# Decay rows of a Mamba-2 mixer copied to all partitions by bf16 products, with its convolutions first, and one bank read early in the mixer before it

## What is computed

```python
proj = h @ w_in                         # (1024, 7432)
ya = swa_sink_attention(...)            # A: sliding window attention
yb = hgrn2_mixer(...)                   # B: gated linear recurrence
yc = mamba2_mixer(...)                  # C: state space model
yd = forgetting_attention(...)          # D
g = jax.nn.sigmoid(gate).reshape(bsz, seq, N_BRANCH, D_MODEL)
merged = g[:, :, 0] * (ya @ w_br_a) + g[:, :, 1] * (yb @ w_br_b) + g[:, :, 2] * (yc @ w_br_c) + g[:, :, 3] * (yd @ w_br_d)
return merged @ w_out
```

```python
conv = causal_conv(xbc, conv_w, width 4, per channel) + conv_b
xbc = jax.nn.silu(conv)                 # 512 channels: xs, bs, cs
a_cum = jnp.cumsum(a * dt, within a chunk)
lmat = jnp.exp(a_cum[l] - a_cum[s])     # for s <= l
y_diag = jnp.einsum('bclhn,bcshn,bhcls,bcshp->bclhp', cc, bc, lmat, xc)
```

## Time and profile before

| | us |
|---|---|
| median of three runs | 2283.86 |
| lowest and highest | 2280.04 and 2293.8 |
| the profiled execution, its own time | 2281.75 |
| its span, first to last instruction | 2280.0 |
| TensorE busy | 2161.1 (95% of the span) |
| VectorE busy | 869.4 (38%) |
| ScalarE busy | 413.2 (18%) |
| GpSimd busy | 590.3 (26%) |
| TensorE's granted clock, mean | 0.979 |

### The profile page before, as it was taken

The page is one execution under the profiler, slowest core; times in us unless marked ns, Lnnn a source line. Parts: engine busy times, 40 slices in busy tenths (PEclk is TensorE's granted clock), DMA queues, the critical chain, the costliest instruction groups (busy, mean ns, idle before and its releaser), DMA issues. The chain is left out here.

```text
span 2280.0 us, 22500 instructions
## 1 busy us (share of the span) xinstructions
PE 2161.1 (95%) x7446; PEld 1146.1 (50%) x7447; DVE 869.4 (38%) x1964; ACT 413.2 (18%) x895; POOL 590.3 (26%) x520
## 2 busy tenths in 40 slices
PE   7999999999989999999999999999999999999990
PEld 4548466557446456544444555444444444444440
DVE  4000024555452323311112666464444444444425
ACT  2100023433422212111111122011111111111112
POOL 0700000122000100012223000355544444454524
PEclk9999999999989999999999999999999999999995
DMA  5411101010211111152213302689999999999953
GB/s 136 138 42 49 40 28 38 28 38 28 66 47 42 65 47 61 32 186 68 70 46 117 124 37 89 263 311 347 343 349 350 352 352 347 342 344 352 335 154 148
DMA packets 126441, 361.93 MB, mean 159 GB/s; under 512 B 33948, under 2 KB 65808, under 8 KB 100896
## 3 DMA queue, kind: packets, MB, share of 16 engines
q1 hardware_dynamic: 100768, 306.35, 36.4%
q0 software_dynamic: 23520, 54.61, 9.5%
q10 hardware_dynamic: 2080, 0.01, 0.1%
HBM read 315.22 MB, written 65.01 MB: 167 GB/s over the span
## 5 line engine op out<-in xcount | busy, mean ns | idle before, releaser
L285 PE MATMUL banks<-arena 128*128 128x512 f32 x1568 | 724.2, 601 | 16.7 <-ACT arena L329 10.5
L2651 PE MATMUL banks<-arena 128*128 128x512 f32 x1056 | 472.2, 600 | 5.7 <-DVE arena L2644 2.8
L285 PEld LDWEIGHTS banks<-arena 128*128 128x128 f32 x1568 | 287.7, 193 | 311.6 <-issue 289.4
L2630 POOL DMA_INDIRECT arena<-h_rows,index x268 | 278.0, 1037 | 340.2 <-DVE index L2616 278.5
L2651 PEld LDWEIGHTS banks<-arena 128*128 128x128 f32 x1056 | 196.4, 191 | 231.6 <-issue 229.8
L2667 PE MATMUL banks<-arena 128*128 128x512 f32 x528 | 242.7, 602 | 1.3 <-ACT arena L2469 0.8
L2667 PEld LDWEIGHTS banks<-arena 128*128 128x128 f32 x528 | 95.4, 190 | 97.3 <-issue 95.6
L1622 PE MATMUL banks<-arena 128*128 128x512 f32 x320 | 141.7, 597 | 2.7 <-DVE arena L1651 2.7
L2638 POOL DMA_INDIRECT sums<-arena,row_to x66 | 109.4, 1657 | 104.1 <-DMA sums<-arena,row_to 54.3
L2644 DVE STREAM_TRANSPOSE arena<-arena 128x1024 f32<-128x1024 f32 x66 | 133.5, 2023 | 6.3 <-PE banks L2651 6.3
L291 PE MATMUL banks<-arena 128*128 128x256 f32 (+1 forms) x640 | 128.0, 359 | 0.0
(11 more groups left out here) (358 smaller groups left out, 2132.4 us busy)
## 6 DMA issues: line engine op xcount, KB each, us to landing
arena<-in_w_exp_gate_dram SPq DMA_DIRECT2D x66, 1024.0 KB, 7.0
arena<-in_w_exp_up_dram SPq DMA_DIRECT2D x66, 1024.0 KB, 10.1
arena<-in_w_exp_down_dram SPq DMA_DIRECT2D x66, 1024.0 KB, 14.0
arena<-in_w_in_dram SPq DMA_DIRECT2D x26, 1024.0 KB, 5.3
gates<-arena SPq DMA_DIRECT2D x48, 256.0 KB, 2.0
arena<-gates SPq DMA_DIRECT2D x48, 256.0 KB, 2.6
arena<-h_rows,index POOLq DMA_INDIRECT x268
arena<-in_x_dram SPq DMA_DIRECT2D x8, 512.0 KB, 5.8
```

The costliest lines, as they stand in the source:

```text
L285: mm = pe.matmul(bank[0:width], w[:, q, col:col + width], g.hT[:, q, at * HALF:(at + 1) * HALF], start=(q == 0), stop=(q == KT - 1))
L2630: return pool.indirect_dma_start(w.x[k][:, 256 * q:256 * (q + 1)], None, rows, bass.IndirectOffsetOnAxis(ap=g.index[:, k, q:q + 1], axis=0 ...
L2651: mm = pe.matmul(g.bank[:, 2, :].rearrange("p (a f) -> p a f", a=2), xT[:, k, :], wgu[:, :, k, :], start=(k == 0), stop=(k == KT - 1))
```

## The change

Four things, all inside `mixers`:

1. In B, `read_beside()` stands ahead of ScalarE's wait for the scans instead of behind it.
2. In C, VectorE makes three of the four convolutions ahead of the decay rows, the fourth behind the selectors. ScalarE reads the first unit before the first tanh, and the second after the third tanh.
3. The decay rows are split by GpSimd into three bf16 pieces whose sum is exact; they lie on partitions 0 to 7, 32 to 39 and 64 to 71 of `pieces`, with zeros between. The selectors are bf16 too, and three times as many.
4. The products at lines 1337 and 1343 become bf16 products over 96 partitions.

```diff
@@ mix_b, scalar
+        read_beside()
         act.wait_ge(scanned, 2)
-        read_beside()
         exps(0)
@@ mix_c
-    sel, sel2 = g.region(at + 4096, 4, P)[0:8], g.region(at + 4608, 2, P)[0:8]
+    sel = g.region(at + 4096, 256).bitcast(BF16).rearrange("p (h n) -> p h n", h=4)
+    sel2 = g.region(at + 4352, P).bitcast(BF16).rearrange("p (h n) -> p h n", h=2)
+    third = (slice(0, 8), slice(32, 40), slice(64, 72))
+    pieces = g.region(R3, HALF).bitcast(BF16)
+    middle, left = g.region(R3 + HALF, HALF).bitcast(BF16)[0:8], g.region(R3 + 1027, T)[0:8]
@@ gpsimd
+        pool.memset(sel[0:96], 0.0).then_inc(s["split"], 1)
+        pool.memset(sel2[0:96], 0.0).then_inc(s["split"], 1)
+        pool.wait_ge(s["conv"], 8)
+        pool.memset(pieces[0:96], 0.0).then_inc(s["split"], 1)
+        pool.wait_ge(s["summed"], 1)
+        pool.wait_ge(s["split"], 3)
+        pool.tensor_copy(pieces[third[0]], dec_rows).then_inc(s["split"], 1)
+        pool.wait_ge(s["split"], 4)
+        pool.tensor_tensor(left, dec_rows, pieces[third[0]], ALU.subtract).then_inc(s["split"], 1)
+        pool.wait_ge(s["split"], 5)
+        pool.tensor_copy(middle, left).then_inc(s["split"], 1)
+        pool.wait_ge(s["split"], 6)
+        pool.tensor_copy(pieces[third[1]], middle).then_inc(s["split"], 1)
+        pool.wait_ge(s["split"], 7)
+        pool.tensor_tensor(pieces[third[2]], left, middle, ALU.subtract).then_inc(s["split"], 1)
+        pool.wait_ge(s["split"], 8)
         pool.wait_ge(s["silu"], 3)
@@ scalar
-        for i in range(4):
+        def tanh(i):
             act.wait_ge(s["conv"], 4 * (i + 1))
             act.activation(th[:, i, :], xc[:, i, :], ACT.Tanh).then_inc(s["tanh"], 1)
-            stage((i + 1) // 2)
+        stage(1)
+        for i in range(3):
+            tanh(i)
+        stage(2)
+        tanh(3)
@@ vector (convolve(i) is the body of the old loop over i)
+        for i in range(3):
+            convolve(i)
         dve.wait_ge(s["z1"], 1)
@@
+        dve.wait_ge(s["split"], 2)
+        for r in third:
+            dve.tensor_copy(sel[r], bcast(g.ident[0:8, 0:4].unsqueeze(2), [8, 4, P])).then_inc(s["sel"], 1)
+            dve.tensor_copy(sel2[r, :, 0:HD], bcast(g.ident[0:8, 0:2].unsqueeze(2), [8, 2, HD])).then_inc(s["sel"], 1)
+            dve.tensor_copy(sel2[r, :, HD:P], bcast(g.ident[0:8, 2:4].unsqueeze(2), [8, 2, HD])).then_inc(s["sel"], 1)
+        convolve(3)
@@ tensor
-        pe.wait_ge(s["sel"], 3)
+        pe.wait_ge(s["sel"], 9)
+        pe.wait_ge(s["split"], 8)
@@
-                mm = pe.matmul(bank[:, 1, h * P:(h + 1) * P], sel[:, h, :], tile(dec_rows, m),
+                mm = pe.matmul(bank[:, 1, h * P:(h + 1) * P], sel[0:96, h, :], tile(pieces, m)[0:96],
@@
-                mm = pe.matmul(bank[:, 2, r * P:(r + 1) * P], sel2[:, r, :], tile(dec_rows, m),
+                mm = pe.matmul(bank[:, 2, r * P:(r + 1) * P], sel2[0:96, r, :], tile(pieces, m)[0:96],
```

More of the change, by code:

```diff
@@ L1125, in mix_c @@
     ss = g.sb("ssC", [P, NT, 2])
-    g.sel_rows = sel
-    names = ("halved z0 z1 z2 z3 z4 nl rowsd keepd summed sel colsT colsr conv tanh silu cpad clear tmT tmr xdt "
+    names = ("z0 z1 z2 z3 z4 nl rowsd keepd summed split sel colsT colsr conv tanh silu cpad clear tmT tmr xdt "
              "rowsb eb0 CB E eb att cdec xdec y u st skip yr gt s1 s2 sq ss sse ssq ssr n1 yT yTr").split()
@@ L1220, in vector, with convolve @@
         dve.tensor_scalar(g.rows[:], g.rows[:], g.rowbias[:], neg_row, ALU.add, ALU.mult).then_inc(s["z1"], 1)
+        dve.tensor_scalar(g.convw[:], g.convw[:], 0.5, None, ALU.mult).then_inc(s["z0"], 1)
+        dve.tensor_scalar(g.convb[:], g.convb[:], 0.5, None, ALU.mult).then_inc(s["z0"], 1)
+        dve.wait_ge(s["z0"], 4)
+        def convolve(i):
+            dve.tensor_scalar(xc[:, i, :], g.cX[:, i, 0:T], g.convw[:, i, 0:1], g.convb[:, i:i + 1],
+                              ALU.mult, ALU.add).then_inc(s["conv"], 1)
+            for t in range(1, 4):
+                dve.wait_ge(s["conv"], 4 * i + t)
+                dve.scalar_tensor_tensor(out=xc[:, i, :], in0=g.cX[:, i, t:t + T], scalar=g.convw[:, i, t:t + 1],
+                                         in1=xc[:, i, :], op0=ALU.mult, op1=ALU.add).then_inc(s["conv"], 1)
+        for i in range(3):
+            convolve(i)
         dve.wait_ge(s["z1"], 1)
@@ L1233, in vector @@
         dve.tensor_tensor_scan(dec_rows, keep, dec_rows, 0.0, ALU.mult, ALU.add).then_inc(s["summed"], 1)
-        dve.tensor_copy(sel, bcast(g.ident[0:8, 0:4].unsqueeze(2), [8, 4, P])).then_inc(s["sel"], 1)
-        dve.tensor_copy(sel2[:, :, 0:HD], bcast(g.ident[0:8, 0:2].unsqueeze(2), [8, 2, HD])).then_inc(s["sel"], 1)
-        dve.tensor_copy(sel2[:, :, HD:P], bcast(g.ident[0:8, 2:4].unsqueeze(2), [8, 2, HD])).then_inc(s["sel"], 1)
-        dve.tensor_scalar(g.convw[:], g.convw[:], 0.5, None, ALU.mult).then_inc(s["halved"], 1)
-        dve.tensor_scalar(g.convb[:], g.convb[:], 0.5, None, ALU.mult).then_inc(s["halved"], 1)
-        dve.wait_ge(s["halved"], 2)
-        for i in range(4):
-            dve.tensor_scalar(xc[:, i, :], g.cX[:, i, 0:T], g.convw[:, i, 0:1], g.convb[:, i:i + 1],
-                              ALU.mult, ALU.add).then_inc(s["conv"], 1)
-            for t in range(1, 4):
-                dve.wait_ge(s["conv"], 4 * i + t)
-                dve.scalar_tensor_tensor(out=xc[:, i, :], in0=g.cX[:, i, t:t + T], scalar=g.convw[:, i, t:t + 1],
-                                         in1=xc[:, i, :], op0=ALU.mult, op1=ALU.add).then_inc(s["conv"], 1)
+        dve.wait_ge(s["split"], 2)
[4 more added lines that the diff above has]
+        convolve(3)
         for i in range(4):
```

## The result

The changed kernel takes 2263.91 us (median of 4 runs, 2263.72 to 2266.67), the kernel before beside it 2285.45 (median of 4, 2280.04 to 2293.8): a ratio of 0.9895, with a 95% interval of 0.9872 to 0.9918. It is 1.05% faster by that ratio; the interval, 0.82 to 1.28%, holds 1% inside it. The two medians are 21.5 us apart, 0.94%.

What follows compares the result with a forecast made beforehand. TensorE, busy for 95% of the span, was taken to bound the kernel. C's head 9.3 plus C's loop 8.7 minus B's 4.1 gave 13.9 us less: 2267.9 profiled, 2270.0 as median, range 2261 to 2277.

Steps and rivals of the forecast that it cites:

- faster by over 1%: Whole kernel: a gain of about 22.8 us, distinguishable from no change; chance 0.04, against 0.93 same and 0.03 slower.
- B, the table load: Mixer B: the exponential's table load falls behind the wait for `gap_min`, so `scores(0)` comes 1.3 us later.
- B, the clock: Mixer B: TensorE idles 446.0 to 454.4, its clock is low when `scores(0)` starts, 2.8 us lost in the open.
- C's head: Mixer C before its loop: 9.3 us gained, 13.0 without GpSimd's split blocking VectorE by 6.5 to 8.3 us.
- Rival 1: No exclusion between GpSimd and VectorE: the split hides, C's head gains 13.0, about 2265 us; chance 0.22.
- The third unit, a wait of 1.8 to 3.6 us near 645: C's head: TensorE's `fill(14)` waits for `stage(4)` to read the third unit, held up by the fourth convolution.
- The second rival: Exclusion, and the clock falls in C: head gains 4.7 to 6.5 us, about 2274 us; chance 0.2.
- The fourth rival: GpSimd slow in bf16: the split takes 25 us, C's head loses 7 to 9, 2287 to 2291 us; chance 0.04.
- Short waits are free: TensorE's waits like the 2.2 us one cost no low clock; so none counted in C's head, 2.8 us if wrong.
- Behind C I count no change: After mixer C: everything hangs on C's end in the same way, so 0 us difference.
- The loop: C's loop: six float32 products per tile become bf16, saving 1.03 to 1.13 us a tile, 8.7 us taken.
- The third rival: C's loop: small bf16 products bound by weight loads, loop saves 0 to 3 us, about 2277 us; chance 0.04.

Runs made afterwards that it cites:

- table free: Changed kernel, early read kept, without the wait for the second scan ahead of B's exponential: 2265.49 us, ratio 0.9911 to the kernel before.
- bf16 only: Changed kernel with C's old order of convolutions and B's read late again; bf16 products and GpSimd split kept: 2283.76 us, ratio 0.9993 to the kernel before.
- filled kernel: Changed kernel with B's filling work redistributed, two units read early, no wait for the second scan: 2250.1 us, ratio 0.9821 to the kernel before.
- Late read: Changed kernel with B's read put back behind the wait for the scans, C's edits kept: 2261.83 us, ratio 0.9905 to the kernel before.
- before again: The kernel before, word for word, profiled a second time: 2287.35 us, ratio 0.9998.
- split on VectorE: Changed kernel with B's read late and the split's five instructions moved from GpSimd to VectorE: 2262.46 us, ratio 0.9881 to the kernel before.
- changed again: The changed kernel, word for word, run once more: 2265.73 us, ratio 0.9900 to the kernel before.
- order only: Changed kernel with float32 decay-row copies, no split, and B's read late; C's new order kept: 2274.87 us, ratio 0.9950 to the kernel before.
- selectors first: Changed kernel with B's read late and the nine selector copies ahead of the decay rows' scan: 2266.83 us beside 2289.56 for the kernel before.
- filled with the split on VectorE: The filled kernel with the split's five instructions moved from GpSimd to VectorE: 2251.57 us, ratio 0.9832 to the kernel before.
- one piece: Changed kernel with B's read late and the split cut to its first instruction, losing precision: 2255.54 us beside 2289.56 for the kernel before.

## Why the prediction was right, and where it was not

The changed kernel took 2263.91 us where I gave 2270.0 and a range of 2261 to 2277. The sign of each of the three terms was right; the sum fell 1.2 us short in the profile, and "faster by over 1%", to which I gave 0.04, can't be told from "the same" (0.82 to 1.28%). That the profile's sum came so close is partly luck: the loop gained 1.8 us more than its term, and D's end lost 1.65 for which I had no term.

**B, the table load: right.** It starts at 449.36 behind line 972, and `scores(0)` comes 1.33 us later; table free takes it back.

**B, the clock: right in size** (3.00 and 3.34 in two profiles, 2.72 in the kernel before with the early read; I had 2.8). The idle time of 8.4 us was 8.53. The row behind it is the earlier trace rows, and the reading that slow entries once covered by a wait would come into the open held.

**C's head: right in size (9.97 against 9.3), wrong in place.** I let VectorE's end move by the split, 6.5 to 8.3 us; it moved by 6.0 (8.2 us for nine copies that take 2.1 alone). But I said that the fourth convolution would grow by some 5 us, and it kept its 3.93: the split was over when it came, because the nine copies, which I had costed at 1.8 us, took all of the blocking. The Trainium skill, "SBUF — State Buffer", "Who interferes with whom", says of copies and casts that they too can take the shared pair, in a mode that uses two ports, and the one that comes second is blocked wholly. I had thought there of instructions with two inputs alone; the trace agrees with this sentence too (0.21 us become 1.05 and 2.01), though no run shows the mode itself. Rival 1 is refuted by bf16 only, where the convolution itself is stretched.

**The third unit, a wait of 1.8 to 3.6 us near 645: not there.** The fourth convolution ended at the early end of where I put it, with B's 3.5 us added (near 648.2), and ScalarE had read the unit at 650.2. TensorE needed it only near 650.4 (twenty entries behind 641.70), because the low clock behind `turn(0)`, for which I had no term, made its filling another 1.7 us later. In the filled kernel, where the clock doesn't fall, the wait appears with 0.89 us. The second rival, in which this wait or the split costs the clock in C, did not come: no low clock follows the 1.22 us before the loop, and the first tile takes 10.01 us like the others.

**The fourth rival, GpSimd slow in bf16: refuted.** The three instructions of the split with one input took 1.15, 1.11 and 1.05 us and the two with two inputs 2.12 and 2.05, where I had taken 1.2 and 2.35 from the float32 rows.

**"Short waits are free": wrong.** I took it from one row, two entries at the usual 1.02 us behind 2.2 us of idle time. Late read and before again have the same instructions and the same wait of 2.21 us; PE's timelines, in the late-read kernel

```profile
608.87 1.02 PE L285 MATMUL banks<-arena 128*128 128x512 f32 x2
...
609.95 1.89 PE L285 MATMUL banks<-arena 128*128 128x512 f32 x2
```

and in the second profile of the kernel before

```profile
608.79 1.02 PE L285 MATMUL banks<-arena 128*128 128x512 f32 x2
...
609.87 1.02 PE L285 MATMUL banks<-arena 128*128 128x512 f32 x2
```

In nine of twelve profiles with this wait the stretch behind it took 8.6 to 8.7 us instead of 6.97, a loss of 1.7; two entries at the usual pace prove nothing, the slow ones may come behind them. The three without the loss all have C's old order and the late read, yet nothing that TensorE or VectorE does differs before the clock falls, so what decides it isn't settled. It costs nothing in the changed kernel's C only because VectorE sets the loop's start there; with the split on VectorE, where nothing else waits, it is in the open.

**"Behind C I count no change": wrong by this too.** D's end has a wait of 1.68 us in every profile. In seven of the fourteen (changed, changed again, table free, order only, bf16 only, selectors first, and filled with the split on VectorE) TensorE's clock falls behind the first or the second such wait, and the stretch from D's first mask product to the next filling entry takes 1.7 to 7.8 us more than the 193.0 of the other seven. D's code is the same in all of them. Both profiles of the changed kernel have it and neither of the two of the kernel before, so it need not be chance from one execution to the next, but what decides it isn't settled either.

**The loop: mechanism right, term too small.** 10.5 us instead of 8.7. Each tile gained 1.33. The six products gained 1.20 instead of 1.03 to 1.13 (0.055 us each, where a quarter of the mask product gave 0.08), and the mask product 0.09, since what follows it is now a bf16 product; the remaining 0.04 are spread. The third rival, bound by weight loads, is refuted.

**The numbers.** The profiled gain is 15.1, the gain of the medians 21.5 in the first comparison and 21.0 in the second. The two profiles lie at different places of their distributions: the one of before 3.7 us below its median, the one of after the longest of its four. I had put the median of before 2.1 us above its profile, from three runs, and let the changed kernel keep the same distance; the comparison moved by 6 us through these distances alone. With that width, a gain of 17 in the profile, within my own forecast, reaches 1% (22.8), and the measured interval lies on both sides of it, so the 0.04 was far too small.

**What stays open.** The kernel before spread over 11 to 16 us in each comparison, the changed one over 3 (ten executions). The low ends differ by 16 us (2279.81 against 2263.72), near the profile's gain; the medians differ by more, because the kernel before reaches higher. The mean granted clock of an execution goes with its length: of the fifty executions of the kernel before beside the experiments, those under 2285 us have 0.978 to 0.981 and those over 2290 have 0.974 to 0.977, while the changed kernel's ten have 0.979 to 0.981. An estimate from these: 0.005 less over 2285 us is some 23 us at the lower level, which costs about 11 us, the size of the spread. So the spread is most likely time at the low clock. Where in the kernel it falls, and whether the long wait in C is the cause, was not shown; D's end alone gave up to 7.8 us in other kernels. Behind the first filling entry after D, the same work in all kernels here took from 1295.7 us (one piece) to 1300.4 (before again), and why is open as well.

## To carry to other kernels

Before work goes to GpSimd because it has time, look at what VectorE does beside it, the short copies included: the copies, the convolution and the products of VectorE were each held when they met an instruction of GpSimd's split, and VectorE did the split in 4.4 us where GpSimd took 7.8. A read or a transfer made early is worth something only with work behind it: alone it turned two waits into a longer one (4.33 us lost in B beside late read, 4.05 in the kernel before without what came behind `turn(0)`), with the filling work spread B gained 9.3. Where an activation with another table follows, look in the built order where the load stands: with two waits ahead of the exponential it went behind the wait for line 972, with one (table free) it ran ahead of it. And compare single profiles stretch by stretch, since a low clock in a stretch that no edit touches made up to 7.8 us here.

## What the runs showed of the chip that I had not expected

- GpSimd's fills don't hold the convolution: the third one kept its 3.93 us at 627.10 beside fills from 627.27 to 628.95. The instruction with one input ahead of it (line 1249) met others and took 1.25 us instead of 0.81.
- A cast of 8x128 elements from float32 to bf16 with one input in SBUF takes 0.21 us alone and 1.05 to 2.01 when it meets a GpSimd instruction; the scalar_tensor_tensor of 128x1024 grows from 1.31 to 2.3 on average, and GpSimd's subtraction from 2.12 to 2.99.
- TensorE's clock fell behind an idle time of 2.21 us in nine of twelve profiles, and behind one of 1.68 us at D's end in seven of fourteen. The low clock may begin 0.4 or 1.4 us behind the wait's end. Behind 1.38 us of idle time and a slow stretch before it the first tile of B took 10.95 instead of 9.28 in two of the seven profiles that have this wait.
- Six bf16 products of 96x128 by 128 columns take 0.33 us, and TensorE begins the one behind the mask product after 0.22 us instead of 0.31 with float32 behind it.
